# A windowed attention core whose scores run one item ahead, with a third probability buffer and the sink as an extra column, and the first layer's last 16 modulation chunks multiplied inside it

## What is computed

```python
sh1, sc1, g1, sh2, sc2, g2 = ada_mods(cond, ada_w[i], ada_b[i])   # silu(cond) @ w + b, 6 x 1024
h = modulate(rmsnorm(x, norm_mix[i]), sh1, sc1)
q, k, v = qkv_proj(h, attn_w_qkv[j], attn_q_norm[j], attn_k_norm[j])
...
def attend_block(qb, keys, values, masks, sink):
    ...
    m = sink_f
    for s in scores:
        m = jnp.maximum(m, jnp.max(s, axis=-1))
    denom = jnp.exp(sink_f - m)
    for s, vp in zip(scores, values):
        p = jnp.exp(s - m[..., None])
        denom = denom + jnp.sum(p, axis=-1)
        out = out + jnp.einsum('bkgqs,bskd->bqkgd', p, vp)
    out = out / jnp.moveaxis(denom, -1, 1)[..., None]
```

## Time and profile before

| | |
|---|---|
| time, median of 3 runs | 2990.75 us (2989.33 to 2991.61) |
| span of the profiled execution, first to last instruction | 2988.2 us |
| the median less this span | 2.55 us |
| busy: PE, PEld | 94%, 89% of the span |
| busy: DVE, ACT, POOL | 54%, 40%, 4% |
| mean granted TensorE clock | 0.971 |

### The profile page before, as it was taken

One profiled execution on the slowest core, in us unless ns is written; L12 is line 12 of the kernel. 1 busy time (PEld: TensorE's weight loads), 2 busy tenths in 40 slices (PEclk: granted clock), 3 DMA queues, 4 the chain that ended last, 5 costly groups with the idle time before them and its releaser, 6 DMA issues.

```text
span 2988.2 us, 51513 instructions
## 1 busy us (share of the span) xinstructions
PE 2801.6 (94%) x19936; PEld 2645.5 (89%) x19936; DVE 1607.8 (54%) x2878; ACT 1184.5 (40%) x2042; POOL 109.7 (4%) x71
## 2 busy tenths in 40 slices
PE   5977799999998999999989999999998779999999
PEld 4965699999998999999969999999997569999999
DVE  2667556625644664366342665366367754663662
ACT  2347445414423552243232543244234754541441
POOL 1000010000002000000201000000100001000000
PEclk7989899999999999999989999999998989999999
DMA  6410133323320332333201332333121002221222
GB/s 233 181 64 1 50 125 134 137 74 135 136 93 33 138 134 103 123 133 130 66 24 57 120 134 100 111 134 127 63 78 36 1 15 61 78 84 64 73 85 74
DMA packets 62431, 279.67 MB, mean 94 GB/s; under 512 B 7392, under 2 KB 9568, under 8 KB 49632
## 3 DMA queue, kind: packets, MB, share of 16 engines
q1 hardware_dynamic: 62304, 277.93, 27.0%
HBM read 274.74 MB, written 3.16 MB: 93 GB/s over the span
## 4 chain that ended last, share of the span: by engine, by line
PE 86%; DVE 6%; ACT 6%; issue 2%; DMA 1%; SPq 0%; POOL 0%; DVEq 0%; ACTq 0%
PE ps L457 73%; ACT prob L923 3%; PE ps L541 3%; PE ps L480 3%; PE ps L743 1%; PE ps L552 1%; DVE prob L1265 1%; DVE prob L1282 1%; PE ps L502 1%; DMA ada_w<-in_ada_w 1%; ACT stat L925 1%; PE ps L680 1%; PE ps L649 1%; PE ps L510 1%; PE ps L635 1%
## 5 line engine op out<-in xcount | busy, mean ns | idle before, releaser
L457 PE MATMUL ps<-h_hi,w_hi 128*128 128x322 f32 x3392 | 799.8, 317 | 7.2 <-DVE w_lo L1057 4.1
L457 PE MATMUL ps<-h_lo,w_hi 128*128 128x322 f32 x3392 | 784.8, 313 | 0.0
L457 PE MATMUL ps<-h_hi,w_lo 128*128 128x322 f32 x3392 | 780.6, 312 | 0.0
L803 ACT ACTIVATE w_hi<-w_raw 128x1024 fp32r<-128x1024 f32 (+1 forms) x288 | 325.5, 1130 | 1037.1 <-PE ps L457 921.1
L457 PEld LDWEIGHTS ps<-h_hi,w_hi 128*128 128x128 f32 x3392 | 569.6, 190 | 34.0 <-issue 28.4
L457 PEld LDWEIGHTS ps<-h_lo,w_hi 128*128 128x128 f32 x3392 | 577.4, 190 | 0.0
L457 PEld LDWEIGHTS ps<-h_hi,w_lo 128*128 128x128 f32 x3392 | 577.0, 190 | 0.0
L1057 DVE TENSOR_TENSOR w_lo<-w_raw,w_hi 128x1024 fp32r<-128x1024 f32 (+1 forms) x288 | 377.3, 1310 | 67.6 <-ACT w_hi L803 65.9
L1177 DVE SCALAR_TENSOR_TENSOR x<-ps,mods,x 128x321 f32<-128x321 f32 (+5 forms) x264 | 99.9, 435 | 537.1 <-PE ps L457 537.1
L457 PE MATMUL ps<-f_hi,w_hi 128*128 128x322 f32 x1408 | 325.1, 312 | 0.0
L457 PE MATMUL ps<-f_hi,w_lo 128*128 128x322 f32 x1408 | 324.5, 312 | 0.0
(11 more groups left out here) (119 smaller groups left out, 2533.1 us busy)
## 6 DMA issues: line engine op xcount, KB each, us to landing
ada_w<-in_ada_w SPq DMA_DIRECT2D x96, 1024.0 KB, 5.5
w_raw<-in_w_in SPq DMA_DIRECT2D x176, 512.0 KB, 3.6
w_raw<-in_w_out SPq DMA_DIRECT2D x64, 704.0 KB, 4.0
w_raw<-in_w_qkv SPq DMA_DIRECT2D x24, 512.0 KB, 5.1
w_raw<-in_w_o SPq DMA_DIRECT2D x16, 512.0 KB, 3.8
w_raw<-in_w_fnet SPq DMA_DIRECT2D x8, 512.0 KB, 3.6
x<-in_x SPq DMA_DIRECT2D x1, 2576.0 KB, 15.5
out_y<-x SPq DMA_DIRECT2D x8, 322.0 KB, 3.7
```

Source lines behind the costliest of these rows:

```text
L457: mm = pe.matmul(ps[:, 2 * par + hf, 0:NH], w[par][:, kk, :], b[:, hf * NH:(hf + 1) * NH], start=(kk == 0 and n == 0), stop=(kk == k - 1 a ...
L803: act.activation(w_hi[par][:, 0:k, :], w_raw[par][:, 0:k, :], ACT.Copy).then_inc(hi_made, 1)
```

## The change

The core's order is new. TensorE makes `scores(0)` ahead of the loop and then `scores(w+1)`, `values(w-2)`, `turn(w-1)` in step `w`. VectorE does `masked(w)` ahead of `normed(w-1)`. `prob` has three buffers (the third, `prob2`, lies where `scaled` lies), each with both heads and 516 columns a head, so that `masked(w)` waits for `turn(w-3)` and no longer for `turn(w-2)`. The sink is a column behind the keys: VectorE makes `sink_col` once (sink times 8), GpSimd copies two numbers a partition into `prob` for each item, and one exponential a head over one column more gives the whole sum. The sink's own exponentials and the addition of line 1279 are gone.

In layer 0, chunks 8 to 23 are made in the core: from item 2 on, an even step ends with `ada_multiply`, an odd one with `ada_turn`. For this the chunks' two PSUM areas share bank 7, and the outputs of all items of layer 0 share bank 6, so `values(w)` waits for `out_lo(w-1)`; in layer 3 it waits for `out_lo(w-2)` as before. SyncE loads chunks 10 to 23, and sends the new keys and values out, after the load for unit 13.

```diff
+            third_prob = sb("prob2", [P, 2, 516], F32, a)
...
-            prob = [[sb(f"prob{s}{hd}", [P, 512], F32, a) for hd in range(2)] for s in range(2)]
+            prob = [sb(f"prob{s}", [P, 2, 516], F32, a) for s in range(2)]
...
+        def chunk_of_work(layer, w):
+
+            c = FIRST_CHUNKS + w // 2 - 1
+            return c if layer == 0 and FIRST_CHUNKS <= c < NCH else None
+
+        def out_bank(layer, w):
+
+            return ps[:, 6 + (w % 2 if layer else 0), 0:P]
...
+                            if w - w0 >= 3:
+                                pool.wait_ge(exp_made, 2 * (w - 2))
+                            if nb == 4:
+                                pool.wait_ge(t_done, 2 * (w - 2))
+                            pool.tensor_copy(prob[w % 3][:, :, end:end + 1].rearrange("p h c -> p (h c)"),
+                                             sink_col[:, a, head:head + 5:4]).then_inc(sink_put, 1)
...
-                    first_layers_chunk(0)
-                    for n in range(1, 12):
-                        if n >= 2:
-                            unit(u0 + n, n % 2, KT, h_tiles, None, (u0 + n) // 2,
-                                 (lambda: sum_heads(layer, n - 3)) if n >= 3 else None)
-                        first_layers_chunk(n)
+                    for n in range(2, 12):
+                        unit(u0 + n, n % 2, KT, h_tiles, None, (u0 + n) // 2,
+                             (lambda: sum_heads(layer, n - 3)) if n >= 3 else None)
                         if n >= 3:
                             turn_heads(layer, n - 3)
-                    if layer == 0:
-                        ada_turn(FIRST_CHUNKS + 11)
-                        pe.wait_ge(ada_done, FIRST_CHUNKS + 12)
...
-                        if w - w0 >= 2:
-                            pe.wait_ge(ol_made, w - 1)
+                        if w - w0 >= 2 or (w > w0 and layer == 0):
+                            pe.wait_ge(ol_made, w - 1 if layer else w)
...
+                    scores(w0)
                     for w in range(w0, w0 + 42):
-                        if w < w0 + 40:
-                            scores(w)
+                        if w + 1 < w0 + 40:
+                            scores(w + 1)
                         if w - w0 >= 2:
                             values(w - 2)
                         if 1 <= w - w0 <= 40:
                             turn(w - 1)
+                        c = chunk_of_work(layer, w)
+                        if c is not None and w % 2 == 0:
+                            ada_multiply(c, c % 2, c // 2, ADA_SHARED)
+                        elif c is not None:
+                            ada_turn(c, ADA_SHARED)
...
+                        act.wait_ge(sink_put, w + 1)
...
-                            act.activation(prob[w % 2][hd][:, lo:hi], prob[w % 2][hd][:, lo:hi], ACT.Exp,
-                                           bias=st[:, 1:2], scale=HD ** -0.5, accum_out=st[:, 2:3])
-                            act.activation(st[:, 3:4], sink[:, a, head:head + 1], ACT.Exp,
-                                           bias=st[:, 1:2]).then_inc(exp_made, 1)
+                            act.activation(prob[w % 3][:, hd, lo:hi + 1], prob[w % 3][:, hd, lo:hi + 1], ACT.Exp,
+                                           bias=st[:, 1:2], scale=HD ** -0.5,
+                                           accum_out=st[:, 2:3]).then_inc(exp_made, 1)
...
-                        if w - w0 >= 2:
-                            dve.wait_ge(t_done, 2 * (w - 1))
+                        if w - w0 >= 3:
+                            dve.wait_ge(t_done, 2 * (w - 2))
...
-                        own.link(dve.tensor_tensor(st[:, :, 4:5], st[:, :, 2:3], st[:, :, 3:4], ALU.add))
-                        own.link(dve.reciprocal(st[:, :, 5:6], st[:, :, 4:5]))
+                        own.link(dve.reciprocal(st[:, :, 5:6], st[:, :, 2:3]))
...
                     for w in range(w0, w0 + 43):
+                        if w < w0 + 40:
+                            masked(w)
                         if 1 <= w - w0 <= 40:
                             normed(w - 1)
-                        if w < w0 + 40:
-                            masked(w)
```

More of the change, by code:

```diff
@@ L365, in _ @@
                         load_units(u0 + n, 1)
-                    if layer == 0 and FIRST_CHUNKS + n < NCH:
-                        load_chunk(FIRST_CHUNKS + n, n % 2, chunk_rows(FIRST_CHUNKS + n))
-                if kind == "attn":
-                    sp.wait_ge(qk_ready, 10 * (a + 1))
-                    sp.wait_ge(qkv_out, 12 * (a + 1))
-                    sp.dma_start(t["new_k"][a], qkv[:, K0:K0 + 2, CTX0:CTX0 + CTX]).then_inc(out_sent, 16)
-                    sp.dma_start(t["new_v"][a], qkv[:, V0:V0 + 2, CTX0:CTX0 + CTX]).then_inc(out_sent, 16)
+                    if layer == 0 and n in (2, 3):
+                        load_chunk(FIRST_CHUNKS + n - 2, n % 2, chunk_rows(FIRST_CHUNKS + n - 2))
+                    if kind == "attn" and n == 13:
+                        sp.wait_ge(qk_ready, 10 * (a + 1))
+                        sp.wait_ge(qkv_out, 12 * (a + 1))
+                        sp.dma_start(t["new_k"][a], qkv[:, K0:K0 + 2, CTX0:CTX0 + CTX]).then_inc(out_sent, 16)
+                        sp.dma_start(t["new_v"][a], qkv[:, V0:V0 + 2, CTX0:CTX0 + CTX]).then_inc(out_sent, 16)
+                        if layer == 0:
+                            for c in range(FIRST_CHUNKS + 2, NCH):
+                                load_chunk(c, c % 2, chunk_rows(c))
                 if layer + 1 < DEPTH and KINDS[layer + 1] == "pool":
@@ L438, in _ @@
                         pool.tensor_tensor(sq_sum[:], sq_sum[:], sq[kk % 2][:], ALU.add).then_inc(sq_added, 1)
+                    if KINDS[layer] == "attn" and not second:
+                        a = layer // 3
+                        w0 = 40 * a
+                        pool.wait_ge(sink_scaled, 1)
+                        pool.wait_ge(qkv_out, 12 * (a + 1))
+                        for w in range(w0, w0 + 40):
+                            nb, tile = WORK[w - w0]
+                            end = KEYS[nb][1] if nb == 4 else 512
+                            head = 8 * (tile // 4) + tile % 4
+                            if w - w0 >= 3:
[4 more added lines that the diff above has]
+                                             sink_col[:, a, head:head + 5:4]).then_inc(sink_put, 1)
         @block.tensor
@@ L532, in turn_heads, with ada_multiply @@
                 turn_back(RMS0[layer] + 1 + i)
-            def ada_multiply(c, par, turn):
+            def ada_multiply(c, par, turn, out=ADA_APART):
                 pe.wait_ge(ada_in[par], turn * 16 + 16)
@@ L566, in _ @@
                 u0 = UNIT0[layer]
-                def first_layers_chunk(n):
-                    c = FIRST_CHUNKS + n
-                    if layer == 0 and c < NCH:
-                        ada_multiply(c, c % 2, c // 2)
-                    if layer == 0 and n and c - 1 < NCH:
-                        ada_turn(c - 1)
                 if explicit(layer, False):
@@ L1288, in out_lo @@
                         dve.wait_ge(oh_made, w + 1)
-                        dve.tensor_tensor(h_lo[:, tile, cols], ps[:, 6 + w % 2, 0:P],
+                        dve.tensor_tensor(h_lo[:, tile, cols], out_bank(layer, w),
                                           h_hi[:, tile, cols].bitcast(F32), ALU.subtract).then_inc(ol_made, 1)
                     for w in range(w0, w0 + 43):
+                        if w < w0 + 40:
+                            masked(w)
                         if 1 <= w - w0 <= 40:
                             normed(w - 1)
-                        if w < w0 + 40:
-                            masked(w)
                         if w - w0 >= 3:
                             out_lo(w - 3)
+                        c = chunk_of_work(layer, w - 1)
+                        if c is not None and w % 2:
+                            ada_copy(c, ADA_SHARED)
+                        elif c is not None:
+                            ada_add(c, 0, CT * c, ADA_SHARED)
                     for n in range(12, 20):
@@ L1305, in _ @@
                         split_next(u0 + n)
-                        c = FIRST_CHUNKS + n
-                        if layer == 0 and c < NCH:
-                            ada_copy(c)
-                        if layer == 0 and 12 < n <= NCH - FIRST_CHUNKS:
-                            ada_add(c - 1, 0, CT * (c - 1))
                 else:
```

51 lines of the change are left out of this document (25 added, 26 removed).

## The result

| | before | changed |
|---|---|---|
| time, median | 2990.04 us (2988.77 to 2991.61) | 2901.26 us (2900.26 to 2902.29) |
| ratio, 95% interval | | 0.9705 (0.9691 to 0.9719) |
| span of the profiled execution | 2988.2 us | 2899.6 us |
| mean granted TensorE clock | 0.971 | 0.978 |

The kernel is 88.8 us faster; 83 were predicted, and 2901 lies inside the range of 2892 to 2936. Each median is of four executions.

A forecast was written before the change was run, and what follows sets the result against it. Engines waiting on each other in a circle were taken to bound the cores, near-full TensorE the projection and output stages. Terms -38 - 14 - 19.3 - 6.7 - 5 = -83 took 2990.75 to 2908 us, range 2892 to 2936.

The forecast's parts named there:

- the circle: In the cores, engines wait on each other in turn, 4.10 us a full item; the new order takes this apart.
- Full items at TensorE's 3.2: Layer 3's core: TensorE becomes the bound of full items, at 3.2 us each for scores, values and turn.
- my 118: Layer 3's core: predicted 118 us against 155.6, a gain of 38.
- The chunks: Layer 0's core: each chunk moved there costs TensorE 1.6 us, 0.8 an item, making full items 4.0.
- my 142: Layer 0's core: predicted 142 us against 156.0, a gain of 14 with the chunks inside.
- Layer 0 outside the core: Layer 0's projection and output stage, freed of chunks, match layer 3's: -19.3 and -6.7 us.
- Costed at nothing: Chunk loads, other queued loads, GpSimd's copy (near nothing) and layer 0's single output bank were taken to add no time.
- its rival: Cores: GpSimd's sink copy is slow, over 4.3 us each, undoing the whole gain; 1% chance.
- The clock, -5: Ends of both cores: tighter context items keep TensorE's clock at 1.00, saving 2.5 us in each attention layer.
- Couplings left: Both cores: strict orders on nearly equal engines cost 0.3 us an item more; +24, about 2932; 20% chance.
- Pauses vanish: Full items: TensorE's 0.17 us pauses disappear once nothing is late; -14, 2894; 12% chance.
- the clock stays at 1.2 GHz: Both cores: TensorE's work takes twice as long, making the kernel slower, about 3120 us; 2% chance.

The follow-up runs named there:

- e1: The changed kernel with only VectorE's old order put back (scaling of the item before ahead of the masked maximum): 2934.58 us.
- e2: The changed kernel with only TensorE's old order put back (scores in their own item's step, not one ahead): 3132.85 us.
- e3: The changed kernel with two probability buffers instead of three, so a masked maximum waits for the turn one item younger: 2975.28 us.
- e11: The changed kernel itself, unaltered, measured again on the same chip as two follow-up kernels: 2902.23 us.
- e5: The changed kernel with layer 0's chunks 8 to 23 back between the projection's and output's units, and two output banks in layer 0: 2906.23 us.
- e8: The changed kernel with a single output bank in layer 3 too, so values wait for the output of the item just ahead: 2906.81 us.
- e10: The changed kernel with layer 0's chunks in items 8 to 39 and needless TensorE products at the end of layer 3's core: 2904.73 us.
- e7: The changed kernel with the context block's eight items first in each core and the latent blocks after them: 2900.01 us.

## Why the prediction was right

**What bounds the kernel, and the circle: right, and shown.** Put back alone, VectorE's order costs 33 us, the scores 232 and the third buffer 74 (e1 to e3). The three are one mechanism: they do not add up, and with VectorE's and the buffers' part but without the scores ahead the kernel is slower than before.

**Full items at TensorE's 3.2: right in kind, 0.08 too high.** They take 3.12. The term that was off is the scores': I took it to the modelled end of their last product (279.92 to 281.06, 1.14) and the others from start to start. From start to start the scores take 1.07 (2285.56 to 2286.63), the values 1.02 (to 2287.65) and the turn 1.03 as priced (to 2288.68), which makes 3.12 of the 3.22. The pauses, "three an item", stayed: the weight loads rest 0.17 ahead of the turn and of the scores, and 0.13 ahead of the values (2286.50 to 2286.63). Sixteen items times 0.08 is 1.3 of the 2.7 us by which layer 3's core (115.3) beat my 118; the two full blocks together took 48.8 where I had 51.2, since their first items went at VectorE's pace, 2.8 to 3.0. Block 3 came out bounded by VectorE and ScalarE, at 2.90 where 2.95 was priced.

**The chunks: the mechanism right, the term mis-sized.** A chunk in the core costs 1.34 (from the pair of items) or 1.39 (22.3/16), not 1.6, and a full item of layer 0 3.79, not 4.0. Sixteen chunks at 0.26 less are 4.2 us, most of the 4.8 between my 142 and 137.2. (By the 135.4 of e11 a chunk costs 1.28.) The 1.6 came from layer 0's projection, and there a chunk does cost about that (19.2/12 in e5, from the same starting point). What makes it dearer between units than between items was not tried.

**Layer 0 outside the core:** -19.3 and -6.7 predicted, -18.6 and -7.7 measured.

**Costed at nothing.** GpSimd's copy takes 0.19 us and is awaited by nobody: right, its rival false. Chunk loads and the other queues show no wait in the core. The single output bank was right only with the third buffer there (e3), and e8 leaves up to 5.6 us open for a core without chunks.

**The clock, -5: wrong in size, and in part in kind.** I took it that the tighter context items would hold the clock up to the output stage. In layer 3 they held it, in layer 0 not even they did (0.50 at 296 to 300, though it was 1.00 there in e11). And I left out the drain behind them, in which TensorE waits for the last items' exponentials (2.61 of 4 us busy): there it fell in layer 3 too. Layer 3's output stage, whose program is the same in both kernels, gained 0.8, and layer 0's 1.0 beyond the chunks' 6.7: 1.8 together in place of 5. Even that is not safe: in e5, with the same layer 3, the output stage took 62.5, as before the change. The price of 2.5 a stage was near: where the clock did stay at 1.00, the stage took 60.2 (e10) and 60.0 (e7, layer 0), 2.1 and 2.3 below the 62.3.

**The sum.** Predicted -38, -14, -19.3, -6.7, -5 for -83; measured -40.3, -18.8, -18.6, and -7.7 and -0.8 for output and clock together, with -2.6 elsewhere and +0.2 in layer 3's projection. Too little for the cores (by 7.1) and too much for the clock (by 3.2) partly cancelled, so that the total came closer than its parts.

**The rivals.** "Couplings left" is false here: TensorE is busy 47.84 of 48 us in full items, with VectorE at 44.91 and ScalarE at 42.38, which is 0.2 and 0.35 us an item less. "Pauses vanish" is false: they stayed, and TensorE stayed the bound. That the clock stays at 1.2 GHz is false in the changed kernel, where it was 1.00 through the full items with their turns. The Trainium skill, TensorE: Matmul & The Clock Gate, section Part 4: PE-mode transpose, says that transposes do not count as busy the same way; the turns are 1.03 of a full item's 3.12 us, and they did not bring the clock down. Whether they count at all is not shown, since two thirds of the time are other products. e2's window at 0.67 shows that a core with an idler TensorE does lose clock.

## What to carry to other kernels

When no engine is full and each waits a little, look for the circle and count what an item costs on each engine alone: the largest count is what a better order can give, and here the chip came within 0.1 us of my count. Order, lookahead and buffers have to change together; one of them missing can leave the kernel slower than before. The worth of a shorter step depends on what bounds at that moment: the sink's column gave 30 us inside the circle and at most 8.5 once TensorE was the bound.

## What the runs showed of the hardware

TensorE's pauses put down to "issue" stand in the row of its weight loads and say little without the row of its products. In a full item the loads rest 0.13 us from scores to values (64x128 tiles to 128x64), 0.17 from values to the turn (to 128x128) and 0.17 from the turn to the scores. After a chunk's product on 128x32 they rest 0.41 ahead of the scores (240.47 in the layer 0 timeline), but its products run until 240.54 all the while:

```profile
239.47 1.07 PE L580 MATMUL ps<-ada_w,cond_act 128*32 128x256 f32 x16
```

After a chunk's turn on 128x128 the loads of the same scores follow at once (236.35). What sets the shorter rests was not tried. A tiny GpSimd copy (128x2) took 0.19 us where an addition of 644 columns took 1.92. The clock's return differs between executions and places of the same program: with short items in front (e7) it stayed at 0.50 for 20 us in layer 3's core, with TensorE busy 14.9 of them, and was back at 1.00 some 12 us into layer 0's.
